# A router fed from x before its layer norm is finished, with the norm's steps moved onto logits and gathered tokens, and another order of filling weight slots

## The chip, the cores and the metric

The kernel runs on one core of a Trainium2 chip. The metric is the device time of one execution in microseconds (us), the median over runs. The engines are PE (TensorE, matmul), DVE (VectorE), ACT (ScalarE), POOL (GpSimd) and SP (SyncE, which here only issues weight transfers).

## The reference, cut to what matters

The model is one hybrid layer (attention, pooling, gated FFN) followed by two layers of a second kind. The change is in the second kind, once per layer. Sizes: 256 tokens, D = 1024, 16 experts of width 512, 2 experts per token.

```python
for l in range(DEPTH_2):                     # 2 layers
    mix = hybrid_mixer(x, w_in[l], ..., w_o[l], pos, slopes, n_keep)   # two attentions, then @ w_o
    x = layer_norm(ALPHA * x + mix, ln1_g[l], ln1_b[l])
    ffn = grouped_moe(x, router_w, router_bias, w_gate[l], w_up[l], w_down[l])
    x = layer_norm(ALPHA * x + ffn, ln2_g[l], ln2_b[l])

# grouped_moe: aff = sigmoid(x @ router_w); the best group of 4 experts, in it the best 2;
#   out = sum over the chosen e of gate_e * ((silu(x @ w_gate[e]) * (x @ w_up[e])) @ w_down[e])
```

All arithmetic is float32. The expert weights are read whole: 16 x 6 MB in each layer.

## The kernel before, in words

Every engine has its own instruction stream, written out by hand, and the streams meet at semaphores. Tokens lie in two halves of 128 partitions. Most products are made from a high and a low part (fp32r), so `feature_major`, `rows_high` and `rows_lo` each split a tile into two.

A layer of the second kind goes through these stages. Input projections; index scores; `turned_a`, the turning of q and k for the first attention; first attention with the top-k steps beside it on DVE; second attention, with the output projection (`out_groups`) in its gaps and after it. Then norm 1 and the router, which is the stretch the change is about. Then sixteen experts in a pipeline (`raise_expert`, `turn_expert`, `lower_expert`, `scatter_expert`), and norm 2.

Norm 1 before: DVE adds x and the projection half by half (`ln_mean`), ACT sums the centred squares, DVE multiplies by the gain (`ln_scale`), POOL takes the root, DVE scales and shifts (`ln_shift`). The normed x is then turned by PE (`feature_major_by_half`), split into `xr` by ACT and DVE, and multiplied with the router weights; 15 products of zeros (`busy(15)`) stand ahead of that on PE. DVE goes through some 16 small steps to `picked`; PE counts (`counted`); DVE builds `one_hot`; PE gathers the tokens of the first four experts (`gather_step`, 32 products), ACT and DVE copy them to `xg`, and the first `raise_expert` starts.

Weights of the experts come as 96 slabs of 1 MB in each layer, numbered m = 0 to 95, into 16 slots (`moe_slots`), slab m into slot m % 16. SP issues them strictly in the order of m (`moe_load`): a slab whose slot is not yet free holds back every slab behind it. For m >= 16 the wait is for `moe_used`, so slab 16 can go when the first half of the first `raise_expert` is done. For m < 16 it is for whatever used that memory before: `slab_used` for the weight rings, `ln_done` for xn, proj and wide_a, `router_logits` for the attention's scratch. After slab 95 of the first layer, SP issues the next layer's first four input weights.

## Time and profile before

| what | us |
|---|---|
| median of 3 runs | 1147.25 (1144.57, 1147.25, 1147.83) |
| the profiled execution, its own time | 1144.47 |
| its span in the trace | 1142.7 |
| PE busy | 1082.2 (95%) |
| DVE busy | 562.1 (49%) |
| ACT busy | 421.1 (37%) |
| POOL busy | 90.0 (8%) |

The span is the time from the first to the last instruction. Busy time of PE is modelled from pipelined matmuls and so is no measure of how near PE is to its peak. The two layers of the second kind behave alike: what happens at t in the first happens at about t + 382 us in the second (slab 16 is issued at 535.94 and at 917.98). The expert stretch runs from about 532 to 748 and from about 914 to 1131.

### The profile page before, as it was taken

What the parts mean: (1) busy time and instruction counts of PE and PEld (TensorE: products, weight loads), DVE (VectorE), ACT (ScalarE), POOL (GpSimd) and SP (SyncE); (2) the same over time, 40 slices, a digit from 0 to 9 for tenths busy, and PEclk for the clock granted to TensorE, in tenths of its full rate; (3) what the DMA queues carried; (4) which work ended last, traced back from release to release, by engine and by line L of the source; (5) the groups of instructions that cost most, each with busy time, mean ns of one, the idle gap of its engine ahead of it and who ended that gap; (6) DMA issues with size and microseconds to landing.
All of it is one profiled execution on the core that took longest, in us unless ns stands there. A gap on an engine that the chain in (4) does not pass through costs nothing.

```text
span 1142.7 us, 16069 instructions
## 1 busy us (share of the span) xinstructions
PE 1082.2 (95%) x6194; PEld 739.6 (65%) x6194; DVE 562.1 (49%) x1060; ACT 421.1 (37%) x755; POOL 90.0 (8%) x115
## 2 busy tenths in 40 slices
PE   7999998999999999898999999989989999999995
PEld 5898988999998797675344443358867634444332
DVE  4764376767667557756222222274784722222224
ACT  5345454555455346633111111143573311111111
POOL 2200000000000012510000000011252000000000
PEclk9999999999999998999999999999989999999998
DMA  8743255564564443349999999943241999999993
GB/s 288 270 148 113 75 175 175 171 201 164 193 207 159 131 132 111 112 165 389 420 421 419 420 420 420 417 158 119 85 171 42 392 390 419 420 420 420 419 420 122
DMA packets 81684, 294.56 MB, mean 258 GB/s; under 512 B 7252, under 2 KB 40386, under 8 KB 56914
## 3 DMA queue, kind: packets, MB, share of 16 engines
q1 hardware_dynamic: 79456, 289.29, 66.2%
q10 hardware_dynamic: 1394, 2.18, 0.5%
q0 software_dynamic: 768, 2.19, 0.5%
q8 instruction: 44, 0.72, 0.3%
q14 instruction: 22, 0.18, 0.0%
HBM read 292.59 MB, written 1.05 MB: 257 GB/s over the span
## 4 chain that ended last, share of the span: by engine, by line
PE 78%; DVE 9%; DMA 5%; ACT 4%; issue 3%; POOL 0%; SPq 0%; DVEq 0%; ACTq 0%
PE bank L2330 16%; PE bank L2339 9%; PE bank L1880 7%; PE bank L1881 7%; PE bank L1882 7%; DMA k_t<-in_w_up 5%; PE bank L1941 4%; PE bank L1943 4%; PE bank L1942 4%; PE bank L1805 4%; PE bank L2317 3%; PE bank L2362 3%; PE bank L1975 2%; PE bank L1959 2%; PE bank L2063 1%
## 5 line engine op out<-in xcount | busy, mean ns | idle before, releaser
L1107 DVE TENSOR_TENSOR lo<-raw,hi 128x2048 fp32r<-128x2048 f32 (+3 forms) x78 | 166.9, 2146 | 62.9 <-ACT hi L695 62.6
L695 ACT CAST hi<-raw 128x2048 fp32r<-128x2048 f32 (+3 forms) x78 | 139.5, 1796 | 60.0 <-PE bank L1882 57.7
L1336 DVE TENSOR_TENSOR proj<-bank,proj 64x512 f32<-64x512 f32 x32 | 34.6, 1082 | 204.5 <-PE bank L2352 192.0
L1941 PE MATMUL bank<-xs,hi 128*128 128x256 f32 x448 | 128.4, 287 | 3.6 <-DVE xs L1137 1.5
L1880 PE MATMUL bank<-hi,xs 128*128 128x512 f32 (+2 forms) x312 | 125.1, 401 | 6.4 <-DVE xs L1141 3.4
L1943 PE MATMUL bank<-xs,lo 128*128 128x256 f32 x448 | 127.5, 285 | 0.0
L1942 PE MATMUL bank<-xs,hi 128*128 128x256 f32 x448 | 127.4, 284 | 0.0
L1881 PE MATMUL bank<-hi,xs 128*128 128x512 f32 (+2 forms) x312 | 119.2, 382 | 0.0
L1882 PE MATMUL bank<-lo,xs 128*128 128x512 f32 (+2 forms) x312 | 118.9, 381 | 0.0
L1045 ACT ACTIVATE proj<-bank 64x512 f32<-64x512 f32 x32 | 18.8, 589 | 202.8 <-PE bank L2331 202.8
L1941 PEld LDWEIGHTS bank<-xs,hi 128*128 128x128 f32 x448 | 86.7, 193 | 5.0 <-issue 3.5
L1942 PEld LDWEIGHTS bank<-xs,hi 128*128 128x128 f32 x448 | 86.7, 193 | 0.4
L1943 PEld LDWEIGHTS bank<-xs,lo 128*128 128x128 f32 x448 | 86.6, 193 | 0.0
L2330 PE MATMUL bank<-moe_w,xg 128*64 128x512 f32 x192 | 85.1, 593 | 1.5 <-ACT xg L1038 1.4
L2331 PE MATMUL bank<-moe_w,xg 128*64 128x512 f32 x192 | 85.2, 593 | 0.0
L1354 DVE SCALAR_TENSOR_TENSOR expert_out<-bank,slot_gate,expert_out 128x512 fp32r<-128x512 f32 x32 | 24.0, 751 | 115.9 <-ACT expert_out L1057 115.9
L588 POOL TENSOR_TENSOR stat<-stat,power 128x1 f32<-128x1 f32 (+2 forms) x15 | 16.5, 1103 | 707.2 <-DVE stat L1738 491.2
L1880 PEld LDWEIGHTS bank<-hi,xs 128*128 128x128 f32 x312 | 60.3, 193 | 16.5 <-DVE lo L1427 3.6
L1057 ACT ACTIVATE expert_out<-bank,slot_gate 128x512 fp32r<-128x512 f32 x32 | 22.0, 687 | 128.8 <-PE bank L2339 128.8
L1882 PEld LDWEIGHTS bank<-lo,xs 128*128 128x128 f32 x312 | 60.4, 194 | 10.7
L1881 PEld LDWEIGHTS bank<-hi,xs 128*128 128x128 f32 x312 | 60.3, 193 | 8.9
L2331 PE MATMUL bank<-raw,xg 128*64 128x512 f32 x144 | 63.9, 593 | 0.0
(286 smaller groups left out, 2096.7 us busy)
## 6 DMA issues: line engine op xcount, KB each, us to landing
raw<-in_w_up SPq DMA_DIRECT2D x40, 1024.0 KB, 5.2
raw<-in_w_in SPq DMA_DIRECT2D x28, 1024.0 KB, 5.3
moe_w<-in_w_gate SPq DMA_DIRECT2D x24, 1024.0 KB, 15.9
moe_w<-in_w_up SPq DMA_DIRECT2D x24, 1024.0 KB, 17.4
moe_w<-in_w_down SPq DMA_DIRECT2D x24, 1024.0 KB, 16.2
raw<-in_w_down SPq DMA_DIRECT2D x19, 1024.0 KB, 5.1
raw<-in_w_gate SPq DMA_DIRECT2D x10, 1024.0 KB, 12.9
raw<-in_w_o SPq DMA_DIRECT2D x8, 1024.0 KB, 4.9
```

The lines of the kernel that those rows point to most:

```text
L695: nc.scalar.copy(high(n)[:, 0:size], raw[:, n % RING, 0:size]).then_inc(S["hi_done"], 1)
L1107: tt(low(n)[:, 0:size], raw[:, n % RING, 0:size], high(n)[:, 0:size].bitcast(F32), ALU.subtract).then_inc(S["lo_done"], 1)
L1805: return nc.tensor.transpose(dst, src, ident[0:src.shape[0], 0:src.shape[0]])
L1880: mm(out_, lhs_hi, rhs_hi, start=first, stop=False)
L1881: mm(out_, lhs_lo, rhs_hi, start=False, stop=False)
L1882: return mm(out_, lhs_hi, rhs_lo, start=False, stop=last)
L1941: mm(dst, wh[:, k, col], x_hi, start=k == 0, stop=False)
L1942: mm(dst, wh[:, k, col], x_lo, start=False, stop=False)
L1943: ins = mm(dst, wl[:, k, col], x_hi, start=False, stop=k == k_chunks - 1)
L2330: mm(to[0:SLOTS, :], rows_[:, kk, :], gate[:, k, :], start=kk == 0, stop=kk == DC - 1)
L2331: ins = mm(to[SLOTS:P, :], rows_[:, kk, :], up[:, k, :], start=kk == 0, stop=kk == DC - 1)
L2339: ins = mm(bank[2][SLOTS * c:SLOTS * (c + 1), :], act[:, kk, :], down[:, k, 512 * c:512 * (c + 1)], start=kk == 0, stop=kk == 3)
```

## The change

The arithmetic of norm 1 is taken apart:

- PE turns x itself, after the addition and before any norm (`turn_x`), into `x_t`, in plain float32. The router weights are multiplied by the gain ahead of time by POOL (`router_gb`), and PE sums these over the features (`gain_sums`, just ahead of the first attention); ACT copies the sums to `route` there. The logits of x times those weights are then corrected for mean, root and shift by two small DVE steps for each half (`logits_normed`).
- x is centred in place by ACT (`centred`); the root goes in as a scale when ACT and DVE split the rows (`rows_high`, `rows_lo`); gain and shift are applied when gathered tokens are copied to `xg` (`with_gains`), by columns kept in `conv`.
- What norm 2 needs of norm 1's output is made later: the gain by four DVE steps (`kept`) beside the first expert, the shift by four products of one row into the accumulator in place of four products of zeros.
- On PE, `turn_x(0, ...)` stands inside the output projection; `busy(15)` is gone and `busy(3)` comes in.
- `moe_slots` is in another order: the attention's scratch and proj come as slots 4 and 5, then two ring slots, xn, and the rest of the rings with q_t and k_t. wide_a, which holds the gain row, is slot 15 and waits for `ln_scaled`, which `kept` raises.

```diff
+        ring_slots = [moe_w[:, RING * part + i, :] for i in (2, 0, 1) for part in range(2)]
         moe_slots = [wide_b[:]] + [raw[:, i, :] for i in range(RING)]
-        moe_slots += [moe_w[:, RING * part + i, :] for i in (2, 0, 1) for part in range(2)]
-        moe_slots += [q_t[:].rearrange("p h t -> p (h t)"), k_t[:].rearrange("p h t -> p (h t)")]
-        moe_slots += [xn[:].rearrange("p a n -> p (a n)"), flat[:, 2 * FFE:2 * FFE + SLAB], wide_a[:]]
-        moe_slots += [attention_slot[:]]
+        moe_slots += [attention_slot[:], flat[:, 2 * FFE:2 * FFE + SLAB]] + ring_slots[0:2]
+        moe_slots += [xn[:].rearrange("p a n -> p (a n)")] + ring_slots[2:]
+        moe_slots += [q_t[:].rearrange("p h t -> p (h t)"), k_t[:].rearrange("p h t -> p (h t)"), wide_a[:]]
...
-                    elif m < RING_SLOT:
+                    elif m < ATTENTION_SLOT:
                         sp.wait_ge(S["lo_done"], b + L_O + 1 + m)
+                    elif m < FIRST_RING:
+                        sp.wait_ge(S["weighted"], 2 * HEADS * (2 * layer + 3))
...
+                    elif m < GAIN_SLOT:
+                        sp.wait_ge(S["slab_used"], b + L_O + 4)
+                    elif m == GAIN_SLOT:
+                        sp.wait_ge(S["ln_scaled"], 2 * HALVES * layer + HALVES)
                     elif m >= MOE_SLOTS:
                         moe_wait(sp, layer, "moe_used", m - MOE_SLOTS + 1)
...
+                w.next("gain_sums")
+                nc.scalar.copy(route[:, 4, :], bank[6][:, sums_at])
                 attention(after=lambda i: split_quarter(b + L_O + (i - 4) // 4, (i - 4) % 4) if 4 <= i < 16 else None)
...
+                for k in range(DC):
+                    ins = mm(bank[6][:, sums_at].rearrange("p (g e) -> p g e", g=2), const[:, C_ONE:C_ONE + 1].broadcast_to([P, P]),
+                             router_gb[:, :, k, :], start=k == 0, stop=k == DC - 1)
+                ins.then_inc(S["gain_sums"], 1)
...
+            def kept(half):
+
+                for c in range(2):
+                    part = slice(512 * c, 512 * (c + 1))
+                    ins = nc.vector.scalar_tensor_tensor(out=x[:, half, part], in0=x[:, half, part], in1=ln_gb[:, 0, part],
+                                                         scalar=stat[:, 2, half:half + 1], op0=ALU.mult, op1=ALU.mult)
+                ins.then_inc(S["ln_scaled"], 1)
...
                 gated_slots(0)
+                w.next("ln_in", 32)
+                for half in range(HALVES):
+                    kept(half)
...
+                column_added(0, 0)
+                column_added(0, 1)
+                variance(0)
+                heads_low(3)
+                turned_odd(0, 0)
+                turned_odd(0, 1)
+                w.next("rstd_ready")
+                rows_lo(0, 0)
+                column_added(1, 0)
+                rows_lo(0, 1)
+                column_added(1, 1)
+                turned_odd(1, 0)
+                variance(1)
+                turned_odd(1, 1)
+                logits_normed(0)
+                w.next("rstd_ready")
+                logits_normed(1)
+                router()
...
+                turn_x(1, 0)
+                turn_x(1, 1)
+                router_products(0, 0)
+                router_products(0, 1)
+                router_products(1, 0)
+                router_products(1, 1)
+                busy(3, bank[2])
+                pe.wait_ge(S["ln_in"], 16 * (4 * layer + 2))
+                pe.wait_ge(S["logits_normed"], HALVES * (layer + 1))
                 for half in range(HALVES):
+                    for c in range(2):
+                        mm(acc[half][c][:], const[0:1, C_ALPHA:C_ALPHA + 1].broadcast_to([1, P]),
+                           ln_gb[0:1, 1, 512 * c:512 * (c + 1)], start=True, stop=False)
                 busy(11, bank[2])
```

In `router()`, one `rows_lo(1, 0)` now stands between `picked` and `place`, and `rows_lo(1, 1)` after the first `slots_of(0)`.

The transfers that SP issues for slabs 4 to 15 of the first layer, before:

```order
L543 DMA moe_w<-in_w_gate_2 128x2048 [waits slab_used]
L543 DMA moe_w<-in_w_up_2 128x2048 [waits slab_used]
L543 DMA moe_w<-in_w_gate_2 128x2048 [waits slab_used]
L543 DMA moe_w<-in_w_up_2 128x2048 [waits slab_used]
L543 DMA moe_w<-in_w_down_2 128x2048 [waits slab_used] x2
L543 DMA q_t<-in_w_gate_2 128x2048 [waits slab_used]
L543 DMA k_t<-in_w_up_2 128x2048 [waits slab_used]
L543 DMA xn<-in_w_gate_2 128x2048 [waits ln_done]
L543 DMA proj<-in_w_up_2 128x2048 [waits ln_done]
L543 DMA wide_a<-in_w_down_2 128x2048 [waits ln_done]
L543 DMA attention_slot<-in_w_down_2 128x2048 [waits router_logits]
```

And the same twelve slabs now:

```order
L571 DMA attention_slot<-in_w_gate_2 128x2048 [waits weighted]
L571 DMA proj<-in_w_up_2 128x2048 [waits weighted]
L571 DMA moe_w<-in_w_gate_2 128x2048 [waits slab_used]
L571 DMA moe_w<-in_w_up_2 128x2048 [waits slab_used]
L571 DMA xn<-in_w_down_2 128x2048 [waits heads_turned]
L571 DMA moe_w<-in_w_down_2 128x2048 [waits slab_used]
L571 DMA moe_w<-in_w_gate_2 128x2048 [waits slab_used]
L571 DMA moe_w<-in_w_up_2 128x2048 [waits slab_used]
L571 DMA moe_w<-in_w_gate_2 128x2048 [waits slab_used]
L571 DMA q_t<-in_w_up_2 128x2048 [waits slab_used]
L571 DMA k_t<-in_w_down_2 128x2048 [waits slab_used]
L571 DMA wide_a<-in_w_down_2 128x2048 [waits ln_scaled]
```

The two earliest slots now go to slabs 4 and 5, and slab 15 waits for `ln_scaled`. The row behind it is slab 16 (wide_b, waits moe_used) in both.

DVE from the copies of the first gathered tokens to the first expert's gating, before:

```order
L1318 TENSOR_TENSOR one_hot<-const,route 128x256
L1371 COPY xg<-bank1 128x4x128 [waits moe_gathered]
L1371 COPY xg<-bank3 128x4x128 [waits moe_gathered]
L415 TENSOR_LOAD rounds [waits rounds_known]
L415 ISA x2
L1327 TENSOR_SCALAR hot_gate<-const,route 128x128 x2
```

And now, where the x<-x,stat,wide_a rows are `kept`, the last of which lets slab 15 go:

```order
L1454 TENSOR_SCALAR xg<-bank1,conv 128x4x64 [waits moe_gathered]
L1454 TENSOR_SCALAR xg<-bank1,conv 128x4x64
L1454 TENSOR_SCALAR xg<-bank3,conv 128x4x64 [waits moe_gathered]
L1454 TENSOR_SCALAR xg<-bank3,conv 128x4x64
L437 TENSOR_LOAD rounds [waits rounds_known]
L437 ISA x2
L1407 TENSOR_SCALAR hot_gate<-const,route 128x128 x2
L1385 SCALAR_TENSOR_TENSOR x<-x,stat,wide_a 128x512 [waits ln_in]
L1385 SCALAR_TENSOR_TENSOR x<-x,stat,wide_a 128x512 x3
L1416 TENSOR_TENSOR proj<-bank0,proj 64x128x4 [waits moe_silu_done]
```

Each copy of 512 columns became two of 256, and four steps of 512 columns came in ahead of the gating.

ACT at the start of the first attention, before:

```order
L993 COPY q_t<-bank0 128x512 [waits turned_a]
L993 COPY q_t<-bank2 128x512 [waits turned_a]
L993 COPY q_t<-bank0 128x512 [waits turned_a]
L785 ACT_TABLE_LOAD [waits flipped]
L785 ACTIVATE prob,row_sum<-logit,row_min 128x128 [waits logits]
```

And now:

```order
L1025 COPY q_t<-bank2 128x512 [waits turned_a]
L1025 COPY q_t<-bank0 128x512 [waits turned_a]
L1029 COPY route<-bank6 128x32 [waits gain_sums]
L817 ACT_TABLE_LOAD [waits flipped]
L817 ACTIVATE prob,row_sum<-logit,row_min 128x128 [waits logits]
```

The table load for the exponential now stands behind a copy that waits for PE's `gain_sums`.

## Rows read from the trace of the kernel before

**Rows 1.** Stretches of the span: engine busy, clock, DMA share, GB/s.

```profile
507.00:535.00 28.00, 25.23 (x145) 16.65 (x145) 21.18 (x56) 10.71 (x15) 3.12 (x6) 1.00 1.01 422
535.00:540.00 5.00, 5.00 (x28) 1.91 (x25) 0.00 (x1) 0.59 (x1) 0.01 (x1) 1.00 0.73 239
540.00:729.00 189.00, 187.61 (x968) 75.14 (x967) 47.70 (x91) 30.12 (x54) 0.00 (x0) 1.00 1.01 420
```

**Rows 2.** Timeline of PE: start, us, line, operation, idle before and its releaser.

```profile
729.40 0.61 PE L2330 MATMUL bank<-q_t,xg 128*64 128x512 f32 x1 [1.12 <-DMA k_t<-in_w_up]
...
1112.02 0.61 PE L2330 MATMUL bank<-q_t,xg 128*64 128x512 f32 x1 [1.32 <-DMA k_t<-in_w_up]
```

**Rows 3.** Timeline of SP's transfer issues in the first layer.

```profile
503.79 0.33 SPq L543 DMA_DIRECT2D moe_w<-in_w_gate  x1
...
522.93 0.33 SPq L543 DMA_DIRECT2D attention_slot<-in_w_down  x1
535.94 0.33 SPq L543 DMA_DIRECT2D wide_b<-in_w_gate  x1
```

**Rows 4.** Timeline from the output products to the gather, several engines.

```profile
507.48 0.39 PE L1880 MATMUL bank<-hi,xs 128*128 128x512 f32 x1
512.33 3.44 PE L1996 MATMUL bank<-zeros 128*128 128x512 bf16 x15
515.61 1.03 PE L1805 MATMUL bank<-const,x 128*128 128x128 f32 x8
510.47 2.25 DVE L1306 TENSOR_TENSOR xs<-x,xs 128x512 fp32r<-128x512 f32 x2 [1.38 <-ACT xs L1021]
509.18 2.37 ACT L1021 CAST xs<-x 128x512 fp32r<-128x512 f32 x2 [3.22 <-DVE x L1759]
523.17 0.18 DVE L1224 TENSOR_SCALAR route<-route 128x32 f32<-128x32 f32 x1
526.46 0.19 DVE L1257 SCALAR_TENSOR_TENSOR picked<-route 128x32 bf16<-128x32 f32 x1
523.72 2.56 PE L1996 MATMUL bank<-zeros 128*128 128x512 bf16 x11
527.18 0.19 DVE L1268 TENSOR_TENSOR route<-route,bank 128x32 f32<-128x32 f32 x1 [0.31 <-PE bank L2307]
528.30 4.01 PE L2317 MATMUL bank<-one_hot,xs 128*128 128x256 f32 x32 [0.35 <-DVE one_hot L1318]
748.59 1.99 PE L2456 MATMUL bank<-value,const 1*128 1x512 f32 x8
```

**Rows 5.** Timeline of DVE at the first expert.

```profile
532.35 0.69 DVE L1371 COPY xg<-bank 128x512 f32<-128x512 f32 x1 [1.19 <-PE bank L2317]
533.28 0.60 DVE L1327 TENSOR_SCALAR hot_gate<-const,route 128x128 f32<-128x128 f32 x2 [0.24 <-issue]
540.00 1.05 DVE L1336 TENSOR_TENSOR proj<-bank,proj 64x512 f32<-64x512 f32 x1 [6.12 <-ACT proj L1045]
505.53 1.41 DVE L1750 SCALAR_TENSOR_TENSOR xn<-x,stat,wide_a 128x512 f32<-128x512 f32 x2
```

**Rows 6.** Timeline at the start of the first attention, PE and ACT.

```profile
484.76 0.52 PEld L1975 LDWEIGHTS bank<-proj,prob_t 128*128 128x128 f32 x4
443.46 0.60 PE L1805 MATMUL bank<-const,wide_b 128*128 128x128 f32 x4
444.93 0.68 PE L1959 MATMUL bank<-k_t,q_t 128*128 128x128 f32 x4 [0.88 <-DVE k_t L1660]
444.26 1.28 ACT L785 ACT_TABLE_LOAD   x1
445.88 0.40 ACT L785 ACTIVATE prob<-logit,row_min 128x128 f32<-128x128 f32 x1 [0.34 <-DVE row_min L1178]
```

**Rows 7.** Stretches for PE alone: busy, clock, DMA share, GB/s.

```profile
444.00:447.00 3.00, 1.80 (x10) 1.00 0.64 161
448.00:454.00 6.00, 5.84 (x24) 0.50 0.50 206
```

More of the change, by code:

```diff
@@ L194, in constants, with gain_columns @@
     c[:, C_IOTA:C_FULL] = np.arange(SLOTS)
-    c[:, C_FULL:C_FOLD] = SLOTS * np.arange(1, SEQ // SLOTS)
-    for part in range(2):
-        c[part * EXPERTS:(part + 1) * EXPERTS, C_FOLD:C_KEPT] = np.eye(EXPERTS)
-    return c
+    c[:, C_FULL:C_ALPHA] = SLOTS * np.arange(1, SEQ // SLOTS)
+    c[:, C_ALPHA] = ALPHA
+    return c
+def gain_columns(gain, shift):
+    both = np.stack([gain, shift]).astype(np.float32)
+    by_chunk = both.reshape(2, LAYERS, DC, P).transpose(3, 1, 0, 2)
+    by_row = both.reshape(2, LAYERS, P, DC).transpose(2, 1, 0, 3)
+    return np.ascontiguousarray(np.stack([by_chunk, by_row], axis=2).reshape(P, GAIN_COLUMNS))
 class Waits:
@@ L651, in _ @@
                     .then_inc(S["kr_spread"], 1)
+                pool.wait_ge(S["columns_in"], 16)
+                pool.wait_ge(S["router_in"], 16 * N_ROUTER)
+                for g in range(2):
+                    nc.gpsimd.tensor_tensor(router_gb[:, g], router_w[:],
+                                            columns[:, layer, 0, g, :].unsqueeze(2).broadcast_to([P, DC, EXPERTS]), ALU.mult)
                 w.next("qup_saved0", 2)
@@ new lines, in rows_high @@
+                def rows_high(half):
+                    act.wait_ge(S["rstd_ready"], ROOTS_EARLIER + ROOTS_PER_LAYER * layer + 2 + half)
+                    w.next("ln_centred", 2)
+                    for i in range(2):
+                        nc.scalar.activation(row_chunks(0, half, i), x_chunks(half, i), ACT.Copy,
+                                             scale=stat[:, 2, half:half + 1]).then_inc(S["rows_hi"], 1)
+                squares_beside(0, 0)
+                squares_beside(0, 1)
@@ L1036, in gathered_step, with with_gains @@
+                centred(1, 1)
+                rows_high(1)
+                w.skip("ln_mean_step", 4)
+                def with_gains(dst, src, chunk):
+                    gain, shift = (columns[:, layer, 1, g, chunk:chunk + 1] for g in range(2))
+                    return nc.scalar.activation(dst, src, ACT.Identity, scale=gain, bias=shift)
                 def gathered_step(g, f, from_):
                     moe_wait(act, layer, "moe_gathered", 4 * g + f + 1)
-                    nc.scalar.copy(xg[:, g % 2, :, 2 * f:2 * f + 2, :],
-                                   from_[:].rearrange("p (c e s) -> p e c s", c=2, e=EPG)).then_inc(S["moe_xg_ready"], 1)
+                    for c in range(2):
+                        ins = with_gains(xg[:, g % 2, :, 2 * f + c, :],
+                                         from_[:, 256 * c:256 * (c + 1)].rearrange("p (e s) -> p e s", e=EPG), 2 * f + c)
+                    ins.then_inc(S["moe_xg_ready"], 1)
@@ L1774, in _ @@
-                w.next("ln_done", HALVES)
-                w.next("router_w_hi")
-                dve.wait_ge(S["router_in"], 16 * N_ROUTER)
-                tt(router_s[:, :, EXPERTS:2 * EXPERTS], router_w[:], router_s[:, :, 0:EXPERTS].bitcast(F32),
-                   ALU.subtract).then_inc(S["router_w_lo"], 1)
-                feature_major(DC, to=xr)
-                rows_lo(1)
-                router()
-                split[0] = b + PER_LAYER
-                earlier = experts(layer, earlier)
+                                                       in1=gain_banks[1][c][:], op0=ALU.mult, op1=ALU.add).then_inc(S[done], 1)
```

305 lines of the change are left out of this document (184 added, 121 removed).

## The prediction

> **What bounds the kernel now.** I read the page first: PE is busy 95% of the span, but the page's DMA line stands near full in the two expert stretches and nowhere else. So I cut the span there and asked for the DMA share and the rate of each stretch. From 540 to 729 us the DMA share is 1.01 and the rate 420 GB/s without a break [rows 1]. One slab is 1.0486 MB, so it costs 2.50 us, and the sixteen experts need 96 of them. Then I asked where PE waits in that stretch. It waits once: 1.12 us in the first layer and 1.32 us in the second, for the up weights of the last expert [rows 2]. That is slab 91. The two streams, PE's and the transfers', run side by side for 190 us and arrive at this slab within about a microsecond of each other, the transfers last.
>
> Last I read the issues of SP [rows 3]. Slabs 4 to 15 go out between 503.79 and 522.93, and slab 16 only at 535.94, when the first half of the first expert is done. The queue has run dry by then: in 535 to 540 the rate is 239 GB/s [rows 1], which leaves (422 - 239) x 5 / 422 = 2.2 us with nothing moved. From there on it is full. So the end of the expert stretch is a sum: the moment at which the queue restarts, which is about 535.94 + 1.7 = 537.6, then slabs 16 to 91, which are 76 x 2.50 = 190.0, makes 727.6, and 1.8 us until PE may use the last: 729.4, as in [rows 2]. What counts for the time is therefore not when the slots are filled, but when the queue restarts after them and how many slabs are then left. The share of 1.01 in 507 to 535 [rows 1] is work that has slack behind it.
>
> **The change part by part.**
>
> *Slots filled earlier.* Slabs 4 and 5 wait for the end of the second attention's products, which I put a few us before 503.79, and most of the others go out as before. If the queue starts at about 502, eleven slabs, 4 to 14, are through by 502 + 11 x 2.5 = 529.5. Nothing is gained by that alone, since slab 16 cannot go before a slot is free. And slab 15 does not go: it is the gain row's slot and waits for `kept`, the four DVE steps behind the first experts' `hot_gate`. SP is strictly in order, so slabs 16 and 17 stand behind it. The queue restarts with slab 15, with 77 slabs up to slab 91 where before there were 76. Price: 2.5 us per layer, plus or minus the shift of the restart.
>
> *When `kept` ends.* Counted from the end of the gather, G (before: 528.30 + 4.01, about 532.3 [rows 4]). DVE copies the last chunk pair as two pieces of 256 columns; a piece of 512 is 0.69 [rows 5], so about 0.75 in all with the delay. Then the load of `rounds`, 0.24, and `hot_gate`, 0.60. Then four steps like those of L1750, which take 1.41 for two [rows 5]: 2.8. Sum 4.5, so SP issues slab 15 at G + 4.5. Before, slab 16 went at G + 3.7. `kept` itself is hidden: DVE stands idle for 6.12 us there [rows 5].
>
> *The way to G.* Before, the output products end at 512.33, then come zeros (3.44), turns, the router products and the fold, and `router()` starts at 523.17 [rows 4]. Now:
> - Eight turns of x enter at 507.48 at 1.03 for eight [rows 4], so the output products end at about 513.3.
> - ACT from 507.9: two copies of 0.35, two centrings of 0.7, two strided splits of 1.2 (two take 2.37 before [rows 4]), to 512.4. DVE follows with its strided split, the first sum of the second half (0.7 + 0.3), the other split, the last sum, to 515.3. PE turns the last four blocks by 515.9.
> - 16 router products in plain float32, which show as two instructions each. The nearest row is L1975, the same 128x128 stationary side: four loads in 0.52, 0.13 each [rows 6]. So 32 x 0.13 = 4.2, to 520.1.
> - Two small DVE steps, the exponential, and `router()` starts at about 521.2: 2.0 us earlier.
> - `picked` comes 3.5 later, as before, at 524.7. PE by then has to do the three zeros, four rows of shift into the accumulator and eleven zeros. The rows go by L2456, eight instructions in 1.99 [rows 4], in place of 0.9; eleven zeros take 2.4. PE is at the counting at 525.1 instead of at 524.8, and DVE has put a split of 1.1 in between, so `place` comes at 526.0 against 527.18 [rows 4]. The second such split lies beside the gather.
> - The gather takes 4.0. G is 531.1, 1.2 earlier than before.
>
> The restart is then at G + 4.5 = 535.6 against 535.94, 0.3 earlier, and the end of the expert stretch comes at -0.3 + 2.5 = +2.2 us in each layer. That is if PE's clock stays at 2.4 GHz. In the trace the clock fell to 1.2 GHz after the thin stretch from 444 to 447, in which PE had only ten short products, and stayed there for more than 6 us [rows 7]. From 513.3 to 520.5 PE now has 8 turns and 32 products of 16 columns, without the fifteen zeros, which held it up. If it falls there, the shift rows and zeros take up to twice their 4.2 us, and most of the 1.2 is lost: +3.3. I take +2.5.
>
> *The sums of the gains.* PE gets eight plain products (sixteen instructions, 0.13 each by the same row, 2.1) between the last turns, which end at 444.0, and the first scores, which start at 444.93 [rows 6]. The first scores move to 446.0, by 1.1. ACT is worse off: its copy of the sums waits to 446.2, and behind it stands the table load, 1.28, that before lay in ACT's idle time [rows 6]. The exponential moves from 445.88 to 447.7, by 1.8. DVE's top-k steps can go on meanwhile, so I take 1.5 per layer; bounds 0.7 (the scores' shift, part of it caught up in the attention) and 2.3. Nothing here can be below zero, as nothing is taken out of that stretch but a router cast of ACT that lay in idle time.
>
> The Trainium skill ("ScalarE: Activation LUTs", What ACT_TABLE_LOAD costs) says that each switch of set costs a drain of 1.38 us besides the load, 2.66 in all. By that the exponential would move by another 1.4, and the sum would be 2.8 us higher. The trace speaks against it here: the load starts 0.02 us after the copy before it, at 444.26 [rows 6], so no drain is seen.
>
> *Hidden.* POOL's two products for `router_gb` lie on an engine that is busy 8% of the span. The gathered copies on ACT are two pieces for one, in a loop in which ACT is busy 30 us of 189 [rows 1]; in the last experts PE has to wait for transfers anyhow, now about 4 us for the 1.1 before, and that is the cover.
>
> The Trainium skill ("DMA: Bandwidth & Descriptors", Anatomy of one DMA) says that a transfer's semaphore wait happens on the issuing sequencer, and that the DMA engines only consume their queues. By that rule slab 15 blocks the sixteen engines as long as `kept` is not done. If waits were taken in the queue instead, the filling of slots would go on around it, and the layer would end 2.5 us earlier than in my sum.
>
> **Sum.** Per layer 2.5 + 1.5 = 4.0, twice is 8.0. Against the profiled execution, 1144.47, that is 1152.5. The three runs of before lie up to 3.4 above it, their median 2.8; I put half of that on top: 1154.
>
> **Rivals.**
> - *The clock falls and stays low.* Both at the router and longer at the start of the attention, where PE's thin stretch grows. Per layer 3.3 + 2.3, and 1 for the half speed in the attention: 6.6, twice 13, so 1159. For it: two stretches of PE are thinner than the one in [rows 7]. Against: zeros remain on both sides of the router. Chance 0.16.
> - *It cancels.* The attention absorbs the shift (0.7), and the router comes a further 1 us earlier than I count, because the products of 16 columns cost less than a row of 64 columns shows. Per layer 1.2 + 0.7, twice 3.8, or less: 1149. Chance 0.20.
> - *Faster.* The transfers do not decide, because slab 15 gets out in time; then PE's own stream does, and each microsecond of an earlier gather is a microsecond of the end. This decides as soon as `kept` ends before the first half of the first expert and G is more than 3.3 us earlier. At G 4.4 earlier, and the 1.1 of waiting gone, a layer is 5.5 shorter and pays 1.5: twice -4.0, so 1138 to 1139. For it: the diff takes some 6 us of work out of the stretch between 512 and 523. Against: DVE, ACT and PE alternate there in a chain that I count step by step. Chance 0.12.
> - *The forecast.* Chance 0.52, with its own range 1150.5 to 1157.
>
> **How the numbers follow.** A measurement of this kernel can tell about 0.3%, 3.4 us, from no change. Slower by more is the forecast nearly whole and the clock's case: 0.66. Within 0.3% is the cancelling case and a little of the forecast: 0.22. Faster: 0.12. The range leaves out the faster case and the far end of the clock's: 1147 to 1160.
>
> **What would show it.** In the transfers of the first layer: dry from about 530 to 537, for 7 to 8 us rather than 2.2, and SP's issue of the wide_a slab and of slabs 16 and 17 together at about 535.6. PE's wait for slab 91 at 3.5 to 5 us instead of 1.1, perhaps over more than one slab. `router()` 2 us earlier against the last output product's old place. The first exponential of each first attention 1.8 us later against the last turned_a, with the table load just ahead of it. I am wrong if slab 15 goes out well before the first expert's first half is done, or if PE's wait for slab 91 is no longer than before.

## The result, and the profile after

The changed kernel takes 1163.87 us (median of 4 runs, 1163.73 to 1164.88), the kernel before 1146.79 in the same comparison: a ratio of 1.0155, 95% interval 1.0137 to 1.0174. It is slower, as forecast, but by 17 us where I had 7, and outside my range of 1147 to 1160. The profiled execution took 1164.88 us with a span of 1163.1 (before: 1142.7), at a mean granted clock of 0.964 against 0.98.

First PE between the router products and the gather, in the first layer; columns as in [rows 4]. It answers to the PE rows there.

```profile
514.47 4.40 PE L2431 MATMUL bank<-router_gb,x_t 128*128 128x16 f32 x32
519.09 1.06 PE L2128 MATMUL bank<-zeros 128*128 128x512 bf16 x2 [0.22 <-issue]
520.08 7.19 PE L2449 MATMUL bank<-wide_a,const 1*128 1x512 f32 x8
527.21 4.31 PE L2128 MATMUL bank<-zeros 128*128 128x512 bf16 x11
531.36 0.17 PE L2457 MATMUL bank<-picked,marks 128*128 128x16 bf16 x1
```

The router products are as priced: 4.40 us against my 4.2. Behind them stand the four shift rows (L2449, each two passes): 7.19 us, where I had 1.99. The eleven zeros take 4.31 instead of 2.4. So the counting products start at 531.36. DVE had the choice of experts ready 8 us before, and waits 7.10 us for them:

```profile
519.78 0.18 DVE L1295 TENSOR_SCALAR route<-route 128x32 f32<-128x32 f32 x1 [0.30 <-ACT route L1094]
...
523.20 0.19 DVE L1328 SCALAR_TENSOR_TENSOR picked<-route 128x32 bf16<-128x32 f32 x1
...
531.74 0.19 DVE L1340 TENSOR_TENSOR route<-route,bank 128x32 f32<-128x32 f32 x1 [7.10 <-PE bank L2461]
...
538.36 2.74 DVE L1385 SCALAR_TENSOR_TENSOR x<-x,stat,wide_a 128x512 f32<-128x512 f32 x4
```

The last row is `kept`, the four multiplies that free the gain row's slot. The stretches of the span tell why PE is slow (columns as in [rows 1], the clock is the third from the right):

```profile
512.00:517.00 5.00, 3.75 (x33) 3.44 (x32) 3.93 (x13) 2.77 (x7) 0.55 (x1) 1.00 1.02 429
...
518.00:530.00 12.00, 11.78 (x22) 4.50 (x23) 4.91 (x19) 3.17 (x4) 0.91 (x2) 0.50 0.84 349
...
531.00:536.00 5.00, 4.65 (x38) 3.70 (x37) 3.99 (x15) 0.68 (x2) 0.00 (x0) 1.00 0.02 5
...
545.00:729.00 184.00, 182.49 (x943) 73.69 (x944) 46.87 (x90) 34.63 (x65) 0.00 (x0) 1.00 1.01 421
```

From 518 to 530 PE runs at 1.2 GHz. From 531 to 536 next to nothing is transferred; the whole dry stretch reaches from about 528 to 542, 14 us where I had 7 to 8. From 545 on the transfers are full again, as in [rows 1]. SP's issues show the dry stretch whole; they answer to [rows 3]:

```profile
512.56 0.43 SPq L571 DMA_DIRECT2D k_t<-in_w_down  x1
541.12 0.33 SPq L571 DMA_DIRECT2D wide_a<-in_w_down  x1
541.50 0.43 SPq L571 DMA_DIRECT2D wide_b<-in_w_gate  x1
541.97 0.43 SPq L571 DMA_DIRECT2D raw<-in_w_up  x1
```

Slab 16 (`wide_b`), right behind slab 15, goes 5.6 us later than the 535.94 of before, although the first slab of the layer went 1.5 us earlier. At the end of the stretch PE waits at three slabs for transfers; the last row answers to [rows 2]:

```profile
721.96 0.61 PE L2484 MATMUL bank<-attention_slot,xg 128*64 128x512 f32 x1 [0.40 <-DMA proj<-in_w_up]
...
731.88 0.61 PE L2484 MATMUL bank<-xn,xg 128*64 128x512 f32 x1 [0.93 <-DMA moe_w<-in_w_up]
...
736.85 0.61 PE L2484 MATMUL bank<-moe_w,xg 128*64 128x512 f32 x1 [1.31 <-DMA moe_w<-in_w_up]
```

Since both layers and many kernels are compared below, I read six moments from each timeline and count them from SP's issue of the layer's first slab. "Sum" is DVE's first sum of half 0 behind the second attention, "choice" its row that writes `picked`, "count" the first counting product, "gather" the first gather product, "slab 16" the issue of `wide_b` behind it, "end" the first gain row product of the second norm.

```
                 layer  sum   choice count gather slab16  end   slab16 to end
before             1   56.9   82.4   82.7   84.2   91.9  304.5  212.6
                   2   56.9   82.3   82.6   84.2   91.8  305.1  213.3
changed            1   57.2   80.6   88.8   90.3   98.9  313.5  214.6
                   2   59.6   84.4   92.9   94.4  102.9  317.5  214.6
```

Layer 1 is 9.0 us longer: 6.1 up to the gather, 0.9 more from there to slab 16, and 2.0 behind it. Layer 2 is 12.4 longer: 10.2, 0.9 and 1.3. Together 21.4; the first slab came 1.5 us earlier and the way between the layers took 0.5 more, which makes the 20.4 between the two spans. (The medians are 17.1 apart, since the profiled execution of before was 2.3 below its median and that of the changed kernel 1.0 above.)

### The profile page after: what moved, and what is told of

It is laid out like the page before. It is cut to its first block, busy times and chain, and to the rows that moved or that the text cites. A ratio compares the mean times of both kernels' runs of the same rounds, so it can differ in the third digit from the quotient of the medians.

```text
span 1163.1 us, 16229 instructions
## 1 busy us (share of the span) xinstructions
PE 1104.2 (95%) x6229; PEld 754.1 (65%) x6234; DVE 560.7 (48%) x1074; ACT 438.3 (38%) x797; POOL 92.0 (8%) x120
## 4 chain that ended last, share of the span: by engine, by line
PE 82%; DVE 6%; DMA 5%; ACT 4%; issue 2%; SPq 0%; DVEq 0%; POOL 0%; ACTq 0%
PE bank L2484 16%; PE bank L2493 9%; PE bank L2012 7%; PE bank L2014 7%; PE bank L2013 7%; DMA moe_w<-in_w_up 5%; PE bank L2073 4%; PE bank L2074 4%; PE bank L2075 4%; PE bank L1937 4%; PE bank L2516 3%; PE bank L2107 3%; PE bank L2471 2%; PE bank L2091 2%; PE bank L2128 1%
## 5 line engine op out<-in xcount | busy, mean ns | idle before, releaser
L2014 PEld LDWEIGHTS bank<-lo,xs 128*128 128x128 f32 x312 | 60.3, 193 | 10.6
```

Of the source, the lines that this page charges most:

```text
L2014: return mm(out_, lhs_hi, rhs_lo, start=False, stop=last)
```

## The experiments

All were measured beside the kernel before on the same chip; its median was 1147.3 us beside runs 1 to 4, 1145.9 beside 5 to 8 and 1146.9 beside 9 to 12, so the ratios are what to compare. Moments and profile lines come from one execution each. The first four runs take PE's lateness apart.

**1. Without the eleven zeros.**

```
-                busy(11, bank[2])
```

> The changed kernel without the eleven products of zeros that stand between the shift rows and the counting products; all else as changed. Theory (TensorE is late ahead of the counting: the choice of experts is there at 523.2 us, the counting starts at 531.4): those zeros took 4.3 us at the granted clock of 0.50 in layer 0 and 4.6 in layer 1, and the whole of it comes off: counting at about 527.1, first gather products 4.3 us earlier, the DMA queue restarted at about 537 instead of 541.1, time about 1164 - 8.9 = 1155. Rival A (the queue's restart, held by the slab behind the multiply by the gain, is what costs, and it does not move with TensorE): counting earlier, SP's issue of slab 15 still at about 541, time 1163 to 1164. Rival B (the zeros end the stretch at 1.2 GHz; without them counting and gather products run at half clock): gather products about 3 us longer, which gives most of it back, 1160 to 1163.

Measured: 1159.5 us, 1.0103 (1.0086 to 1.0120). Count at 85.2 and 84.7, so 3.6 earlier than in the changed kernel in layer 1, and 8.2 in layer 2, where this profile also had the clock low for a shorter time. Slab 16 came only 2.4 earlier in layer 1: the first gather products now ran at the low clock, and the gather took 5.13 us where the changed kernel has 4.01. Theory right in direction, with rival B taking a third of it back. Rival A falls: slab 16 moved with PE.

**2. The shift rows replaced by zeros.**

```
                 for half in range(HALVES): for c in range(2):
-                    mm(acc[half][c], const[0:1, C_ALPHA..], ln_gb[0:1, 1, ..], start=True, stop=False)
+                open_acc()
```

> The changed kernel with the four products that put the shift row into the sums' banks replaced by four bf16 products of zeros, as the kernel before opened them (the shift is left out of what is kept); eleven zeros and all else as changed. Theory (shift rows, not only the clock, make TensorE late): 8 passes took 7.2 us in layer 0; four zeros at half clock take about 1.6, so counting 5 to 5.6 us earlier, time about 1164 - 11 = 1153 (1152 to 1155). Rival A (choice of experts at 523.2 us on VectorE is the later one once the rows are gone): zeros would end at 520.1 + 1.6 + 4.3 = 526.0, still later than 523.2, so this one gives the same unless the clock recovers. Rival B (queue's restart independent of TensorE): 1163.

Measured: 1153.3 us, 1.0054 (1.0037 to 1.0070), as the theory said. Count at 83.4 and 85.0. The kernel leaves the shift out of its result, so it only prices the rows: put in place of zeros, they are worth 10.6 of the 17 us. That holds a part of the clock's cost too. Between the turns and the gather the clock was low for about 7 us in both layers here, for 13 and 17 in the changed kernel.

**3. The clock held by zeros in the thin stretch.**

```
                 turn_x(1, 0)
+                busy(6, bank[6])
                 turn_x(1, 1)
+                busy(4, bank[7])
                 router_products(0, 0); router_products(0, 1)
+                busy(4, bank[7])
                 router_products(1, 0); router_products(1, 1)
```

> The changed kernel with 14 products of zeros in the thin stretch: six between the two batches of transposes of half 1, four ahead of the router's products, four between those of half 0 and half 1; eleven zeros and shift rows as changed. It is to hold the granted clock at 1.00 from 512 to 531 us, where the changed kernel shows 0.50 from 517.4. Theory 1 (clock alone: a row at full clock costs the 0.25 us a pass that the gain rows showed): router products end 1.8 us later at about 520.7, rows 2.0, eleven zeros 2.4, counting at about 525.8 instead of 531.4, time about 1164 - 11 = 1153. Theory 2 (the rows of one row group run one after the other, 0.45 us a pass at 2.4 GHz): rows 3.6, counting at about 527.4, time about 1164 - 8 = 1156. Rival (the clock falls all the same): everything 1.8 us later a layer, time about 1167.

Measured: 1158.3 us, 1.0100 (1.0084 to 1.0117). PE in the second layer, and the clock beside the rows:

```profile
911.91 3.81 PE L2452 MATMUL bank<-wide_a,const 1*128 1x512 f32 x8
915.66 4.04 PE L2128 MATMUL bank<-zeros 128*128 128x512 bf16 x11
```

```profile
912.00:915.00 3.00, 3.00 (x8) 1.28 (x8) 2.63 (x13) 2.91 (x4) 0.91 (x2) 1.00 1.00 415
...
916.50:918.00 1.50, 1.50 (x5) 0.59 (x4) 0.42 (x1) 0.00 (x0) 0.00 (x0) 0.50 1.00 415
```

This is the price at a granted clock of 1.00: the eight passes take 3.81 us, 0.48 each, not 1.99. Theory 2 holds for the rows. The clock did not hold to the end, though: between 915 and 916.5 its mean is 0.60, so it fell with the last of the rows, and in the first layer it fell some 1 us into them (rows 6.19, zeros 4.87). So only part of the expected gain came, 5.5 us of the 8.

**4. The rows on two row groups.**

```
-   pool.dma_start(ln_gb[0:1, 1, :], shift.unsqueeze(0))
+   pool.dma_start(ln_gb[0:33, 1, :], shift.partition_broadcast(33))
...
+   row = slice(32 * c, 32 * c + 1)
-   mm(acc[half][c], const[0:1, C_ALPHA..], ln_gb[0:1, 1, ..], ...)
+   mm(acc[half][c], const[row, C_ALPHA..], ln_gb[row, 1, ..], ...)
```

> The changed kernel with the shift loaded to partitions 0 to 32 and the four row products alternating between partition 0 (columns 0 to 511) and partition 32 (columns 512 to 1023), so that neighbours use two row groups of TensorE, as two of the gain rows of the second norm do; all else as changed. Theory (passes on one row group follow each other, those on two run side by side): 8 passes 3.6 to 4.2 us instead of 7.2 at the half clock, counting 3.0 to 3.6 us earlier, time about 1164 - 6.5 = 1157.5. Rival (0.89 us is what such a pass costs at 1.2 GHz whatever the row group): 7.2 us again, time 1164.

Measured: 1156.1 us, 1.0071 (1.0055 to 1.0088), as the theory said. The same eight passes at the same low clock:

```profile
523.89 3.78 PE L2450 MATMUL bank<-wide_a,const 1*128 1x512 f32 x8
527.60 4.32 PE L2128 MATMUL bank<-zeros 128*128 128x512 bf16 x11
```

7.19 became 3.78. In the changed kernel the passes of the rows start one at a time, 0.85 us apart; here they start in pairs, one of each row group.

The Trainium skill ("TensorE: Matmul & The Clock Gate", Why this matters for your kernels) says that products of small K run at once if their operands lie at partitions 32 apart, and that a single one is no cheaper than a full one. This run agrees with the first half, by 1.90, and no run here tests the second.

The row by which I had priced the shift, L2456 in [rows 4], had its operands on partitions 0 and 32 as well.

**5. Both: two row groups, and the thin stretch filled**, this time by taking half 0's router products ahead of half 1's last turns, with four zeros behind.

```
                 turn_x(1, 0)
-                turn_x(1, 1)
                 router_products(0, 0); router_products(0, 1)
+                turn_x(1, 1)
+                busy(4, bank[7])
                 router_products(1, 0); router_products(1, 1)
```

> The changed kernel with the shift rows alternating between partitions 0 and 32 (as in the run that did this alone) and with the thin stretch filled: half 0's sixteen router products moved ahead of the second four transposes of half 1, then four products of zeros ahead of half 1's router products; eleven zeros as changed. Theory (late TensorE = serial rows times low clock, and the clock is the work of the thin stretch): granted clock 1.00 up to the counting, rows 1.9 to 2.0 us, zeros 2.4, counting about 7 us earlier than in the changed kernel against the first expert slab's issue (88.8 us after it there, so 82), time 1164 - 14 = 1150. Rival (the row products themselves bring the clock down: they are the last thing ahead of its fall in the run with fourteen zeros): clock falls during or right after the rows, zeros at 4.3 us, counting at about 84 to 86, time 1153 to 1156.

Measured: 1152.2 us (1143.6 to 1155.4), 1.0047 (1.0025 to 1.0070). The profiled execution took 1147.9, the second fastest of ten, so its moments flatter the version. PE in the first layer:

```profile
519.51 1.99 PE L2451 MATMUL bank<-wide_a,const 1*128 1x512 f32 x8
521.43 4.24 PE L2128 MATMUL bank<-zeros 128*128 128x512 bf16 x11
```

The rows now take the 1.99 us of my forecast. The clock fell right behind them all the same, as the rival has it, so the zeros took 4.24; the count still came at 81.6 in both layers, where theory had 82. Slab 16 was at 91.8, exactly where it is in the kernel before, and yet the layers ended 3.4 and 1.2 us later. In the first layer 1.49 of the 3.4 are a gap of PE just ahead of the end, in which it waited for nothing that the profile shows, and that no run explains:

```profile
751.45 0.39 PE L2139 MATMUL bank<-zeros 128*128 128x512 bf16 x1 [1.49 <-issue]
```

The rest is the subject of the next run.

**6. The gain row's slot freed early.** Only DVE's order changes, and SP waits in addition for the counting, which stands behind the last reader of the shift row.

```
                 logits_normed(0)
+                kept(0)
                 logits_normed(1)
...
                 rows_lo(1, 0)
+                rows_lo(1, 1)
+                kept(1)
                 w.next("counted")
```

> The changed kernel with the four multiplies by the gain (which free the gain's slot) taken forward on VectorE: half 0's between the two halves' logits, half 1's ahead of the wait for the counting, so that slab 15 goes out when the counting products are done instead of 8 us after the first gather product. TensorE's work is untouched. Theory (the order of the slots costs a seventy-seventh slab of 2.5 us after the restart, and up to 0.9 us because the restart waits for the multiply instead of the first expert's products): slab 15 issued about 89 us after the first slab instead of 98.5, slab 16 at about 98, end of the layer 3.3 us earlier, time 1164 - 6.6 = 1157. Rival (the queue is not what sets the end; TensorE and its clock alone are): gather products as before, time 1163 to 1164.

Measured: 1160.0 us, 1.0129 (1.0101 to 1.0156). SP in the first layer:

```profile
535.04 0.33 SPq L572 DMA_DIRECT2D wide_a<-in_w_down  x1
543.68 0.33 SPq L572 DMA_DIRECT2D wide_b<-in_w_gate  x1
544.05 0.43 SPq L572 DMA_DIRECT2D raw<-in_w_up  x1
```

Slab 15 went out beside the count, slab 16 7.5 us behind the first gather product (changed kernel: 8.6; before: 7.7), and from slab 16 to the end it took 213.6 instead of 214.6. So the slot order costs 1.1 + 1.0 = 2 us a layer. The time fell by 3.9, but over 1158.6 to 1163.6, with a ratio whose interval overlaps the changed kernel's; the moments carry the claim. That stretch is 213.6 in both layers here and 213.7 to 214.1 in runs 8, 9 and 12, which free the slot early too; in the changed form with the slot freed late it is 214.2 to 214.6 (but for the gap in run 5). The theory had 3.3 a layer: a slab less behind the restart is worth 1.0 of its 2.5 us here, and why not more no run tells (in the kernel before, the 5 us behind the restart move 239 GB/s [rows 1], so some of it may lie in that ramp). The rival falls.

**7. The copy of the sums behind the first steps of the attention.**

```
-                w.next("gain_sums")
-                nc.scalar.copy(route[:, 4, :], bank[6][:, sums_at])
+                    if i == 3: (the same two lines, beside the attention's step 3)
```

> The changed kernel with ScalarE's copy of the gain sums out of their bank moved from ahead of the first attention's first exponential to behind its fourth step; the sixteen sum products stay where they are. Theory of the forecast (the copy and the table load behind it hold up the first exponential, and the attention is later by that, 1.1 to 1.8 us a layer): first half's sum 1.1 to 1.5 us earlier against the first slab, time 1164 - 2.5 = 1161.5. Rival (the delay is taken up inside the attention, since half 0's sum stood 57.2 us behind the first slab against 56.9 in the kernel before): time 1163 to 1164.

Measured: 1164.3 us, 1.0156 (1.0133 to 1.0178): nothing. The forecast's 1.5 us a layer is not to be had by moving the copy, and the rival holds. The sixteen products stayed in front, so this run says nothing about their share.

**8. Joined:** runs 4, 5 and 7 together, and:

```
-                busy(11, bank[2])
+                busy(7, bank[2])
                 logits_normed(0)
+                kept(0)
...
                 rounds_needed()
+                kept(1)
```

> The row products on two row groups, the thin stretch filled, the copy of the sums moved back, seven zeros instead of eleven, and the multiplies by the gain taken forward: half 0's between the two halves' logits, half 1's behind the count of rounds, ahead of the shares. If the terms add up as the theory has them: counting about 81.5 us after the first slab, gather at 83, slab 15 at 86 without a dry stretch, slab 16 at 91.5, one slab less behind the restart than the changed kernel; layer end 1 to 2 us earlier than in the kernel before, time 1144 to 1147. If the clock falls all the same, counting at about 84.5 and time 1149 to 1152. If the slot order does not matter, 1149.

Measured: 1146.0 us, 0.9994 (0.9980 to 1.0008), as expected: the whole loss is made up for. The profiled execution, 1143.2, is the fastest of ten. Count at 78.5 and 79.3, 2 to 3 us earlier than expected, slab 16 at 89.9 and 90.6, end at 303.6 and 304.6, only 0.9 and 0.5 ahead of the kernel before. The clock was 1.00 through both stretches of the first layer:

```profile
444.00:458.00 14.00, 12.10 (x75) 8.88 (x74) 12.38 (x63) 12.09 (x42) 4.80 (x5) 1.00 0.34 123
508.00:530.00 22.00, 19.38 (x123) 14.15 (x122) 18.18 (x56) 12.37 (x21) 1.46 (x3) 1.00 1.00 409
```

**9. Joined, with DVE's shares and second one-hot rows behind the gathered copies.**

```
                 kept(1)
-                shares()
-                slots_of(1)
                 (copies of the gathered tokens)
+                shares()
+                slots_of(1)
```

> The joined version with VectorE's shares and the second group's one-hot rows moved behind the copies of the gathered tokens, so that the multiply of half 1 stands in their place. In the joined version the first expert waited 1.55 us for VectorE's gathered copy, and slab 16 went out 9.3 us after the first gather product instead of 7.7. Theory: slab 16 at 88.5 us after the first slab instead of 90.2, layer end 1.5 us earlier, time 1146 - 3 = 1143. Rival (the second group's gather waits for its one-hot rows, now later): a new wait of TensorE of about 1 us behind the first expert, but slab 16 as said, since its slot comes free before; time the same 1143. Rival (slab 16 does not move the end): 1146.

Measured: 1142.3 us (1136.3 to 1146.4), 0.9952 (0.9935 to 0.9968), faster than both. The mean granted clock over its runs is that of version 8, 0.979 in both, so the step between them is not the clock's. Slab 16 goes 7.9 and 7.7 us behind the first gather product (joined: 9.3 and 9.2). The profiled execution, 1146.4, is the slowest of twelve: the clock fell in the first attention of both layers and in layer 1 once more ahead of the count, and the first layer was 2.3 us longer than the second (end at 306.3 and 304.0). The spread goes with the clock: the three runs at a mean of 0.984 or 0.985 took 1136.3 to 1138.0, those at 0.972 to 0.978 took 1142.3 to 1146.4.

**10. The kernel before, without the fifteen zeros.**

```
-                busy(15, bank[2])
```

> The kernel before without its fifteen products of zeros behind the output projection, all else as before. Theory (those zeros kept the clock at 1.00 through the norm; the changed kernel lost it with them): the granted clock falls to 0.50 some microseconds behind the projection's end, about 518 us in layer 0, transposes and router products of the router take up to twice as long, counting 1 to 4 us later than 82.7 us after the first slab, time 1149 to 1155. Rival (the changed kernel loses the clock for another reason, its narrow products of 16 columns or its one-row products): clock stays at 1.00, time 1147.

Measured: 1149.7 us, 1.0026 (1.0014 to 1.0038).

```profile
514.00:517.00 3.00, 0.79 (x8) 0.55 (x6) 2.90 (x9) 1.21 (x2) 0.00 (x0) 1.00 1.01 426
517.00:523.00 6.00, 4.05 (x18) 3.68 (x19) 4.86 (x10) 3.56 (x7) 0.56 (x1) 0.51 1.01 422
524.50:530.00 5.50, 4.48 (x26) 2.34 (x28) 3.81 (x19) 0.49 (x2) 0.92 (x2) 1.00 1.00 417
```

The clock falls at 517 here too, without row products or products of 16 columns. The zeros had held it. PE was busy for 0.79 of the 3 us ahead of this fall, though, and in the changed kernel for 3.75 of the 5 ahead of its own, so whether the narrow products count as work for the clock there this run does not tell. Count at 83.9, 1.2 later: the fall costs the old kernel little, for it lasted 6 to 7 us there, in the first 6 of which PE was busy for 4.05, and no rows lay in it.

**11. The sums beside the attention's steps.**

```
-                (sixteen products, ahead of the attention)
+                (one pair after each of the steps 1 to 8; the copy at step 10)
```

> The changed kernel with the sums of gain and shift taken apart into the first attention: one of the eight product pairs after each of the steps 1 to 8, and ScalarE's copy at step 10; nothing of them stands ahead of the first scores. Theory of the forecast (1.87 us of products and the copy ahead of the attention delay it by 1.5 us a layer): half 0's sum at 55.7 to 56.5 us after the first slab where runs of the changed form show 56.4 to 59.6, time 1164 - 3 = 1161. Rival (the attention's length goes by its clock, not by the sums): half 0's sum 56.4 with the clock at 1.00 and 58 or more where it falls, as with the sums in front; time within 1 us of 1164 apart from that.

Measured: 1167.7 us, 1.0194 (1.0170 to 1.0218), slower than the changed kernel (1163.9; the intervals of the two ratios just overlap). Half 0's sum came at 60.1 in both layers. The attention's start, first layer:

```profile
443.00:448.00 5.00, 3.93 (x26) 2.97 (x26) 4.56 (x20) 3.47 (x8) 1.14 (x2) 0.97 0.48 136
449.00:461.00 12.00, 12.00 (x51) 11.12 (x51) 7.22 (x36) 7.94 (x29) 4.65 (x4) 0.50 0.11 43
```

Nothing of the sums stood ahead of the scores, and the attention was the longest of all, because the clock was 0.50 for 12 us. The forecast's theory falls; the rival's mechanism holds, though it did not foresee that the move would lose time.

**12. Version 9, with the sums beside the steps and ten zeros among them.**

```
+                        busy(3 if i == 1 else 1, bank[7])
```

> The version with the shares moved, plus the sums beside the attention's steps, plus ten products of zeros there (three after step 1, one after each of steps 2 to 8). If the zeros hold the clock at 1.00 at the attention's start in both layers and fit into TensorE's waits there: half 0's sum at 56 us after the first slab in both layers, time 1 to 3 us below the version without them, 1140 to 1142. If the zeros do not fit into the waits: up to 2.2 us later a layer, 1146 to 1148.

Measured: 1141.9 us (1140.4 to 1143.1), 0.9960 (0.9944 to 0.9976). The clock and the first layer's restart:

```profile
443.00:461.00 18.00, 16.00 (x110) 12.96 (x111) 15.85 (x73) 14.81 (x48) 6.16 (x6) 1.00 0.27 95
508.00:530.00 22.00, 20.57 (x130) 15.27 (x130) 16.61 (x50) 10.88 (x18) 1.47 (x3) 1.00 1.00 413
```

```profile
530.09 0.33 SPq L571 DMA_DIRECT2D wide_a<-in_w_down  x1
534.80 0.33 SPq L571 DMA_DIRECT2D wide_b<-in_w_gate  x1
```

The median is that of version 9, within what can be told; the six runs spread over 2.8 us, the twelve of version 9 over 10.1. The moments of the runs that the argument rests on:

```
                 layer  sum   choice count gather slab16  end   slab16 to end
1 no eleven        1   58.0   81.2   85.2   86.8   96.5  311.1  214.5
                   2   57.2   80.6   84.7   86.2   95.8  310.1  214.4
2 zeros for shift  1   58.0   81.4   83.4   84.9   93.6  307.9  214.4
3 clock            1   56.4   80.7   87.9   89.5   98.1  312.7  214.6
                   2   57.9   82.1   86.2   87.7   96.3  310.9  214.6
4 two row groups   1   57.9   81.3   86.0   87.5   96.2  310.4  214.2
5 both             1   57.2   79.2   81.6   83.1   91.8  307.9  216.1
                   2   57.8   79.7   81.6   83.2   91.8  306.3  214.5
6 kept early       1   58.0   81.3   89.5   91.0   98.5  312.1  213.6
7 copy late        1   57.6   80.9   89.1   90.6   99.2  313.6  214.4
                   2   57.0   82.2   90.2   91.7  100.3  314.9  214.6
8 joined           1   56.2   78.2   78.5   80.6   89.9  303.6  213.7
9 shares late      2   57.8   79.8   80.1   82.3   90.0  304.0  214.0
10 before, no zeros 1  57.0   83.5   83.9   85.4   92.9  305.8  212.9
11 sums beside     1   60.1   82.7   91.4   92.9  101.5  316.1  214.6
12 all             1   56.7   78.7   79.0   81.2   88.9  302.6  213.8
```

## Why the prediction was wrong

The step that failed is "PE is at the counting at 525.1". Counted from the first slab (444.09 before, 442.58 after) that is 81.0 us, and it came at 88.8; what lay behind it followed. (The 1.5 us priced for the sums of the gains would put it at 82.5; only 0.3 of them came in this layer.) The parts of a layer show that this is where the forecast broke. Up to half 0's sum it had +1.5, measured +0.3 and +2.7 in the two layers. From there to the gather it had -1.2, measured +5.8 and +7.5. Behind the gather it had +3.3, measured +2.9 and +2.2.

**The shift rows (priced 1.99, measured 7.19).** The mechanism was in the forecast, and so was the clock; what was wrong is the base price. I took L2456 because the shape is the same, one partition by 512 columns in float32, and did not see that its operands lie on two row groups, partitions 0 and 32. Those of L2449 all lie on partition 0. Run 3 gives 3.81 at full clock, so the row was 1.8 us too cheap; the low clock doubles what it finds, another 3.4. Even on two row groups 1.99 is no fixed price. In the kernel before, the passes of L2456 start in pairs, the pairs some 0.43 us apart. In the changed kernel's first layer the same gain rows run one pass at a time, 0.43 us apart, with a break after the fourth, at a granted clock of 1.00:

```profile
756.05 3.57 PE L2611 MATMUL bank<-value,const 1*128 1x512 f32 x8
```

**The clock.** I said that, if it falls, "shift rows and zeros take up to twice their 4.2 us, and most of the 1.2 is lost". It did fall, at about 517, and stayed low for 13 us in the first layer and 17 in the second. Rows and zeros took 11.5 us where 4.4 was in the sum: 1.8 more for the rows' base, 3.4 and 1.9 for the clock on rows and zeros, 7.1 together. The rows also started 0.9 later than my sum had them (77.5 us after the first slab, against 81.0 - 4.4 = 76.6). That is the 7.8, within 0.2. Run 10 shows that the fifteen zeros which the change took away had held the clock in the kernel before. (My "4.2" for rows and zeros was a slip; 1.99 and 2.4 make 4.4.)

**The dependent end.** The rest of the way was right: `router()` was 2.0 us earlier by my sum and 1.9 by the trace (519.78 against 523.17, less the 1.5 by which the layer lies earlier), and the choice came 80.6 us after the first slab, as I had it. I put PE's arrival at 525.1 beside a choice at 524.7, 0.4 us apart, and gave a range to neither. With so little slack any error of PE's goes to the end whole.

**Slab 15 behind `kept`.** The mechanism was right: slabs 15, 16 and 17 went out together within 0.9 us, and 77 slabs follow the restart. The size was not: behind the gather I had 0.8 us for the restart at G + 4.5 instead of G + 3.7 and 2.5 for the slab, 3.3 a layer. The table has 2.9 and 2.2, and run 6 gets 2 of them back. I also said that PE's wait for slab 91 would be 3.5 to 5 us, and that I am wrong if it is no longer than before. It is hardly longer, 1.31 against 1.12, and 1.32 in both kernels' second layer; but the wait is spread over three slabs, 2.6 us in all, and the 1.5 more of it agrees with the 1.3 to 2.0 of the table. The sign was chosen badly: PE starts as late as the transfers do, so its wait does not show a late restart.

**The sums of the gains.** Predicted 1.5 us a layer, bounds 0.7 and 2.3, and "nothing here can be below zero". The first exponential did come 1.4 later against the first slab. Half 0's sum came 0.3 later in the first layer and 2.7 in the second. Seven profiles have the same code up to there, the changed kernel and runs 1 to 6. In their fourteen layers it stands at 56.4 to 59.6, on average 57.8, which is 0.9 later than the 56.9 of before. Its place goes with the clock. Where that was low for about 10 us up to there, as in the kernel before, the sum came at 57.2 to 57.8; where it was low for 3, at 56.4; for 14, at 57.9 or 58.0; for 17, at 59.6. So at an equal clock the term is 0.3 to 0.9 us, and the rest, of either sign, is the clock's. Moving the sums beside the steps did not help: in run 11 the clock was low for 17 us in both layers, which with the sums in front happened in two of fourteen. Run 12, with zeros among them, has 56.7 and 56.9.

**Rivals.** "The clock falls and stays low" at 1159 was nearest, and it had a chance of 0.16. It was too cheap by the rows' base price, which a low clock doubles, and too dear for the sums in the first layer.

What stays open is what makes the clock fall in one execution and not in another. Runs 5 and 8 do the same work on PE from the router products to the end of the shift rows; in the first it fell right behind them, in the second it did not. Versions 8 and 9 do the same at the attention's start, and there it fell in 9 alone. So a single profile with the clock at 1.00 is no proof that the filling held it, version 12's neither; its narrower spread speaks for that, but rests on six runs. All profiles together do show that the filling works on the stretch at the router. Without it (changed kernel, runs 1, 2, 4, 6, 7, 11) the clock fell ahead of the place of the shift rows in all fourteen layers. With it (runs 3, 5, 8, 9, 12) it never did: it fell during the rows or right behind them in five of ten layers, and not at all before the gather in the other five.

## What to carry to other kernels

Before a row of the trace is used as a price, look at where its operands lie: the same shape on one row group or on two differed by a factor of 1.9 here, and on two only where passes of both were under way together. Work that is "only there to keep the clock" is part of the price of whatever follows it; when a change removes it, double everything of PE up to the next busy stretch, and place the sum against the next engine's arrival. A slot whose release hangs on off-path work does not belong in the middle of an in-order queue, unless that work is moved to where its engine idles: here two multiplies in a gap of 2 us, and two in place of work that could wait.

## What the runs showed of the hardware

- Products of one partition by 512 columns in float32, two passes each: 0.48 us a pass at a granted clock of 1.00, 0.90 at 0.50, all on one row group; 0.25 and 0.47 where neighbours alternate between two (runs 3, 4, 5 and the changed kernel). On two groups whose passes did not overlap, 3.57 us for eight at 1.00 (changed kernel, 756.05).
- The clock fell to 0.50 in stretches in which PE counts as busy: in run 5, 8.85 of the 9 us from 512 to 521 were busy at 1.00, with products of 16 columns and rows of one partition the last of them, and it was 0.50 from 522.
- It was 0.50 for 13 us in the changed kernel's first layer, where 7.19 of them were row products, and for about 3.4 us in run 5, where the rows lay ahead of the fall and zeros behind it.
- ACT's table load began 0.01 us behind the copy of the sums (444.29 + 0.18, then 444.48), and the exponential 0.02 us behind the load (444.48 + 1.28, then 445.78), again without a drain.
